# A one-core decoder kernel: clearing the gather buffer in two earlier parts, and storing each tile of h ahead of the preceding tile's normed rows

## The chip, the cores and the metric

The kernel runs on one core of one Trainium2 chip. The metric is the device time of one execution in microseconds (us). TensorE (PE) does the matmuls, VectorE (DVE) and ScalarE (ACT) the work on elements, GpSimd (POOL) issues the indirect transfers that gather and scatter rows, and SyncE (SP) issues nearly all other transfers. The engines run apart and meet only at semaphores. All arrays are float32 unless a name says otherwise.

## What is computed

Two layers over 512 positions of 1024 channels. Layer 0 mixes by windowed attention and a short convolution, layer 1 by trailing means; each mixer is followed by a mixture of 16 experts, of which a position uses two. Cut to what matters here:

```python
for layer in range(2):
    u = rms_norm(h, norm_mix[layer]) * (1 + sc1) + sh1
    h = h + g1 * mix(u)                       # attention + convolution, or pooling
    u = rms_norm(h, norm_ffn[layer]) * (1 + sc2) + sh2
    h = h + g2 * grouped_moe(u, ...)          # sigmoid scores, best group, top 2 of it
return rms_norm(h, norm_final)
```

```python
def grouped_moe(h, ...):
    scores = sigmoid(h @ w_router)            # 16 experts in 4 groups
    ...                                       # best group, its two best experts, gates
    for e in range(16):
        hid = silu(t @ w_gate[e]) * (t @ w_up[e])
        out = out + gates[:, e:e + 1] * (hid @ w_down[e])
```

## The kernel before

The 512 positions are T = 4 tiles of 128 partitions. `h` holds the residual in SBUF, `xhat` the rows divided by their root mean square. In each layer the work goes: mixer, norm, router, routing, expert loop, adding back.

**Mixer and norm.** In layer 0 TensorE multiplies attention and convolution outputs by `w_out` (`mix_half(t, a)`, tile t, half a of the columns, 16 matmul records each) and raises `mix_banked` after each half: it reads 6 when tile 2 is done and 8 when tile 3 is. VectorE adds a half to `h` (`mix_in`, L1033 and L1034); with the second half of a tile it raises `h_ready`. In layer 1 `pool_in` (L1049) does this. ScalarE sums the squares of the finished row (`norm`, L708), VectorE or, for the last tile in layer 0 and the last two in layer 1, ScalarE (`last_tile`, L745) scales it into `xhat` and raises `xhat_ready`.

**Stores.** SyncE writes both `h` and `xhat` to device memory (`h_dram`, `xhat_dram`), since the experts' rows are gathered from `xhat_dram` and their outputs added into `h_dram`. It does so tile by tile (L499 to L502), in the order of its program: it waits for `xhat_ready`, stores the tile of `h`, then the tile of `xhat`, 512 KB each. `xhat_stored` counts the `xhat` stores that have landed. POOL issues no gather before all four have.

**Routing.** `route(l)` on VectorE starts with a CAST of token numbers into a bfloat16 table (L1190), waits for ScalarE's sigmoid (L743), and goes through a chain of short operations (L1194 to L1224) to the choice of experts. TensorE turns that into positions (L1809); `one_hots` (L1312) and `tokens` (L1322, L1331) make the list of rows of the first experts and raise `table_ready`. `keep_clock` (L1547) are matmuls on constants whose result nobody reads, put between these steps.

**Gather.** POOL gathers an expert's rows from `xhat_dram` into one of four buffers of `xg` (L626, indirect, up to 128 rows); row numbers out of bounds write nothing, so `xg` is cleared once, by a MEMSET of 128x4096 (L594) behind the loads of the modulation vectors (`load_gate`, `load_cols`, L554 to L564), which POOL issues once `h_ready` counts four tiles. `xg` lies in the same SBUF columns of `work` as `convT` and `attnT`, the left operands of the mix: column block t*128 to (t+1)*128 of each of their eight rows of 512 is what the mix of tile t reads.

**Expert loop.** TensorE transposes the gathered rows (`turn_in`, L1854), ScalarE (L847) and VectorE (L1394) copy them out with scale and shift, TensorE multiplies (L1877, L1915). Expert weights come through four slots, freed as TensorE goes on; those of experts 0 and 1 are loaded ahead, the rest only when VectorE has sorted the experts (`ids_ready`). In layer 0 SyncE in addition waits for the gather of expert 1. Outputs are scattered (L613, L607) into `h_dram`.

Of the kernel before, what the change touches and what calls it, by code (L numbers as in the profile page):

```python
# [30 lines left out]
P = 128  # L31
SEQ, D = 512, 1024
T = SEQ // P
# [44 lines left out]
def trunk(nc, x, c, w_ada, b_ada, norm_mix, norm_ffn, w_in, w_out, sinks, conv_w, w_pool, pool_scale,  # L78
          w_router, b_router, w_gate, w_up, w_down, norm_final, consts, pool_mats, out, mod_dram, xhat_dram, h_dram):
    ctx = ExitStack()  # L80
    with ctx:
        ctx.enter_context(nc.allow_non_contiguous_dma(reason="vectors of 1024 channels, 128k + p at partition p"))

        def sb(name, shape, dt=F32):
            return ctx.enter_context(nc.sbuf_tensor(name, shape, dt))

        def sem(name):
            return ctx.enter_context(nc.semaphore(name))


        h = sb("h", [P, T, D])
        xu = sb("xu", [P, 2 * T * D])
        xhat = xu[:, 0:T * D].rearrange("p (t d) -> p t d", t=T)
# [37 lines left out]
        def take(n):  # L131
            at[0] += n
            assert at[0] <= WORK, at[0]
            return work[:, at[0] - n:at[0]]
# [18 lines left out]
        xg = take(4 * D).rearrange("p (b d) -> p b d", b=4)  # L153
# [120 lines left out]
        std_done, xhat_ready = sem("std_done"), sem("xhat_ready")  # L274
        xhat_stored = sem("xhat_stored")
# [5 lines left out]
        h_part, h_ready = sem("h_part"), sem("h_ready")  # L281
# [11 lines left out]
        mix_banked = sem("mix_banked")  # L293
# [7 lines left out]
        xg_clear = sem("xg_clear")  # L301
# [6 lines left out]
        h_stored = sem("h_stored")  # L308
# [105 lines left out]
        def _(sp):  # L414
# [81 lines left out]
            sp.dma_start(psc, pool_scale.partition_broadcast(P).rearrange("p a d -> p (a d)")).then_inc(wpool_in, 16)  # L496
            for l in range(LAYERS):

                for t in range(T):  # L499
                    sp.wait_ge(xhat_ready, (2 * l + 1) * T + t + 1)  # L500
                    sp.dma_start(h_dram[l][t * P:(t + 1) * P, :], h[:, t, :]).then_inc(h_stored, 16)
                    sp.dma_start(xhat_dram[l][t * P:(t + 1) * P, :], xhat[:, t, :]).then_inc(xhat_stored, 16)  # L502
                if l == 0:

                    sp.wait_ge(mix_banked, 2 * T)
                    load_expert(0, 1, 1, parts="g")
                if l == 0:

                    sp.wait_ge(xg_in[1], 16)

                sp.wait_ge(xhat_stored, 16 * T * (l + 1))
                sp.wait_ge(logits_ready, 2 * (l + 1))
                sp.wait_ge(ids_ready, l + 1)
                chosen = {}
                for e in range(FIXED, E):
                    chosen[e] = sp.value_load(ids[0:1, e - FIXED:e - FIXED + 1], min_val=0, max_val=E - 1)
                    if e < NSLOT:
                        load_expert(l, e, e % 4, chosen[e])
                        continue

                    load_expert(l, e, e % 4, chosen[e], parts="gu")
                    if e > NSLOT:
                        load_expert(l, e - 1, (e - 1) % 4, chosen[e - 1], parts="d")
                load_expert(l, E - 1, (E - 1) % 4, chosen[E - 1], parts="d")
                overflow_sync(sp, l)

                for j in range(2):
                    sp.wait_ge(y_out[j], 16 * SCATTERS[j] * (l + 1))  # L528
                for t in range(T):
                    sp.dma_start(h[:, t, :], h_dram[l][t * P:(t + 1) * P, :]).then_inc(h_in[t], 16)  # L530
                if l == 0:

                    for t in range(T):
                        sp.wait_ge(h_in[t], 16 * 2)
                    for e in range(FIXED):
                        load_expert(1, e, e)
# [7 lines left out]
        def _(pool):  # L544
            def load_cols(s):

                l, half = s // 2, s % 2
                mod_waits(pool, PIECES.index((l, 3 * half + 1)))
                off = 3 * half * D

                for a in range(s == 2, 2):
                    src = mod_dram[l, off + a * D:off + (a + 1) * D]
                    src = src.rearrange("(k p) -> p k", p=P) if s == 2 else src.rearrange("(p k) -> p k", k=KD)
                    pool.dma_start(modc[:, s, a, :], src).then_inc(modc_in[s], 16)  # L554
                if half:

                    for a in range(2):
                        pool.dma_start(modk[:, l, a, :], mod_dram[l, off + a * D:off + (a + 1) * D]
                                       .rearrange("(k p) -> p k", p=P)).then_inc(modc_in[s], 16)

            def load_gate(l, half):
                off = (3 * half + 2) * D
                mod_waits(pool, PIECES.index((l, 3 * half + 2)))
                pool.dma_start(gbc[:, :] if half else gmix[l], mod_dram[l:l + 1, off:off + D].partition_broadcast(P)  # L564
                               .rearrange("p a d -> p (a d)")).then_inc(gbc_in, 16)
# [11 lines left out]
            for l in range(LAYERS):  # L577
                if l == 0:
                    load_cols(1)

                pool.wait_ge(h_ready, T * (l + 1))
                load_gate(l, 1)
                if l:
# [7 lines left out]
                    load_gate(1, 0)  # L591

                if l == 0:
                    pool.memset(xg[:, :, :], 0.0).then_inc(xg_clear, 1)  # L594
                    pool.wait_ge(xg_clear, 1)
                pool.wait_ge(xhat_stored, 16 * T * (l + 1))

                def scatter(e):
# [1506 lines left out]
```

## Time and profile before

| what | value |
|---|---|
| three timed runs, median | 689.59 us |
| lowest and highest of them | 689.57 and 692.98 us |
| profiled execution, its time | 691.79 us |
| its span, first to last instruction | 690.1 us |
| mean granted clock of TensorE | 0.965 of full |
| TensorE busy | 636.4 us, 92% |
| VectorE busy | 358.3 us, 52% |
| ScalarE busy | 171.5 us, 25% |
| POOL busy | 96.9 us, 14% |
| gather of expert 0 issued, layer 0 and layer 1 | 273.57 us and 499.98 us |

Start times count from the start of the span of the profiled execution. The profiled execution lies 2.2 us above the median of the timed runs, and 1.7 us of its time lie outside its span. TensorE is near full but for two stretches of some 15 us, from 264 and from 490 us, where routing runs on VectorE and the gathers are awaited.

### The profile page before, as it was taken

What the parts mean: (1) busy time and instruction counts of PE and PEld (TensorE: products, weight loads), DVE (VectorE), ACT (ScalarE), POOL (GpSimd) and SP (SyncE); (2) the same over time, 40 slices, a digit from 0 to 9 for tenths busy, and PEclk for the clock granted to TensorE, in tenths of its full rate; (3) what the DMA queues carried; (4) which work ended last, traced back from release to release, by engine and by line L of the source; (5) the groups of instructions that cost most, each with busy time, mean ns of one, the idle gap of its engine ahead of it and who ended that gap; (6) DMA issues with size and microseconds to landing.
All of it is one profiled execution on the core that took longest, in us unless ns stands there. A gap on an engine that the chain in (4) does not pass through costs nothing. (4 is left out here: it accounts for less than half of the span.)

```text
span 690.1 us, 8415 instructions
## 1 busy us (share of the span) xinstructions
PE 636.4 (92%) x2897; PEld 328.6 (48%) x2897; DVE 358.3 (52%) x714; ACT 171.5 (25%) x437; POOL 96.9 (14%) x84
## 2 busy tenths in 40 slices
PE   4899989999899995889999999999678999999994
PEld 3455434444444442445455554468345455555441
DVE  4117698799996237863432222264776233223325
ACT  5000322323333421211122211242421122122223
POOL 0010001000000004113132312100021212222210
PEclk9999989999999996989999999999989999999997
DMA  9999998878889415799999998374789899999726
GB/s 326 361 367 371 384 318 289 328 263 293 311 307 393 160 64 186 249 410 312 322 345 371 359 321 272 92 274 183 305 304 393 278 309 354 370 367 364 253 41 244
DMA packets 68568, 203.76 MB, mean 295 GB/s; under 512 B 9633, under 2 KB 18965, under 8 KB 68524
## 3 DMA queue, kind: packets, MB, share of 16 engines
q1 hardware_dynamic: 58836, 183.63, 72.3%
q0 software_dynamic: 9040, 18.87, 11.4%
q10 hardware_dynamic: 648, 0.71, 0.3%
q8 instruction: 24, 0.39, 0.2%
q14 instruction: 20, 0.16, 0.1%
HBM read 189.90 MB, written 23.11 MB: 309 GB/s over the span
## 5 line engine op out<-in xcount | busy, mean ns | idle before, releaser
L1877 PE MATMUL ps<-ring,work 128*128 128x512 f32 x288 | 127.8, 595 | 0.0
L949 DVE SCALAR_TENSOR_TENSOR acc<-adaw,cond,acc 128x1024 f32<-128x1024 f32 x70 | 89.8, 1283 | 8.5 <-DMA adaw<-in_w_ada_dram 6.6
L1701 PE MATMUL psY<-xu,ring 128*128 128x512 f32 x192 | 88.0, 612 | 0.0
L1877 PEld LDWEIGHTS ps<-ring,work 128*128 128x128 f32 x288 | 54.3, 191 | 67.1 <-issue 66.8
L1402 DVE TENSOR_TENSOR work<-work,ps 128x256 f32<-128x256 f32 (+1 forms) x32 | 11.9, 372 | 128.6 <-ACT work L854 92.7
L854 ACT ACTIVATE work<-ps 128x256 f32<-128x256 f32 (+1 forms) x32 | 11.0, 344 | 237.7 <-PE ps L1877 175.6
L1915 PE MATMUL psY<-ring,work 128*128 128x512 f32 x144 | 69.8, 630 | 0.0
L1701 PEld LDWEIGHTS psY<-xu,ring 128*128 128x128 f32 x192 | 36.4, 195 | 45.4 <-issue 45.2
L613 POOL DMA_INDIRECT h_dram<-work x20 | 33.2, 1662 | 152.7 <-DVE work L1432 75.4
L847 ACT ACTIVATE work<-psA,modc,scl 128x128 f32<-128x128 f32 (+1 forms) x120 | 42.5, 434 | 48.2 <-PE psA L1854 46.6
L1432 DVE SCALAR_TENSOR_TENSOR work<-psY,work,gbc 128x512 f32<-128x512 f32 x40 | 28.2, 747 | 44.1 <-PE psY L1915 44.1
L1394 DVE TENSOR_SCALAR work<-psA,scl,modc 128x128 f32<-128x128 f32 (+1 forms) x120 | 37.8, 377 | 14.9 <-PE psA L1854 13.3
L626 POOL DMA_INDIRECT work<-xhat_dram,work x32 | 34.6, 1081 | 67.9 <-DVE work L1331 33.0
L1760 PE MATMUL psY<-ring,work 128*128 128x512 f32 x96 | 42.8, 597 | 0.8 <-DVE h L1034 0.8
L1915 PEld LDWEIGHTS psY<-ring,work 128*128 128x128 f32 x144 | 27.6, 202 | 28.9 <-issue 28.6
L1854 PE MATMUL psA<-cst,work 128*128 128x128 f32 (+1 forms) x240 | 34.3, 281 | 5.2 <-DMA work<-xhat_dram,work 5.2
L1854 PEld LDWEIGHTS psA<-cst,work 128*128 128x128 f32 (+1 forms) x240 | 30.7, 196 | 10.8 <-DMA work<-xhat_dram,work 7.0
L564 POOL DMA_DIRECT2D gbc<-mod_dram x3 | 1.7, 572 | 219.3 <-DVE h L1034 140.7
L791 ACT ACTIVATE work<-work,sm 128x256 f32<-128x256 f32 (+1 forms) x32 | 15.0, 471 | 52.6 <-DVE sm L1116 52.6
L1760 PEld LDWEIGHTS psY<-ring,work 128*128 128x128 f32 x96 | 17.7, 190 | 21.8 <-issue 21.8
L708 ACT ACTIVATE work<-h 128x1024 bf16<-128x1024 f32 x19 | 20.0, 1050 | 14.3 <-DVE h L1357 12.6
L1868 PE MATMUL ps<-ring,work 128*64 128x256 f32 x192 | 23.0, 390 | 0.0
(266 smaller groups left out, 782.1 us busy)
## 6 DMA issues: line engine op xcount, KB each, us to landing
adaw<-in_w_ada_dram SPq DMA_DIRECT2D x84, 512.0 KB, 5.3
ring<-in_w_gate_dram SPq DMA_DIRECT2D x48, 512.0 KB
ring<-in_w_up_dram SPq DMA_DIRECT2D x48, 512.0 KB
ring<-in_w_down_dram SPq DMA_DIRECT2D x48, 512.0 KB
xu<-in_w_gate_dram SPq DMA_DIRECT2D x16, 512.0 KB
xu<-in_w_up_dram SPq DMA_DIRECT2D x16, 512.0 KB
xu<-in_w_down_dram SPq DMA_DIRECT2D x16, 512.0 KB
work<-in_w_ada_dram SPq DMA_DIRECT2D x12, 512.0 KB, 9.9
```

The source lines that it names most:

```text
L613: pool.indirect_dma_start(out=h_dram[l], out_offset=bass.IndirectOffsetOnAxis(tok_i[:, e:e + 1], 0), in_=yrow[:, e % 2, :], in_offset=None ...
L626: pool.indirect_dma_start(out=xg[0:rows, e % 4, :], out_offset=None, in_=xhat_dram[l], in_offset=bass.IndirectOffsetOnAxis(tok_i[0:rows, e ...
L847: ins = act.activation(xgT[:, j % 2, k, 0:n], turned_ps(e)[:, k * P:k * P + n], ACT.Identity, scale=scl[:, 2 * l + 1, k:k + 1], bias=modc[ ...
L949: dve.scalar_tensor_tensor(total, adaw[:, n % ABUF, :], cond[:, k:k + 1], total if k else brow[:, :], ALU.mult, ALU.add).then_inc(mac_step, 1)
L1394: ins = dve.tensor_scalar(xgT[:, j % 2, k, 0:n], turned_ps(e)[:, k * P:k * P + n], scl[:, 2 * l + 1, k:k + 1], modc[:, 2 * l + 1, 0, k:k + 1],
L1432: ins = dve.scalar_tensor_tensor(yrow[:, j % 2, cols], psY[:, cols], gslot[:, bass.ds(e, 1)], gbc[:, cols], ALU.mult, ALU.mult)
L1701: ins = pe.matmul(bank, wt, uT[:, k, :], start=(k == 0), stop=(k == KD - 1))
L1760: ins = pe.matmul(ps[:, a * 512:(a + 1) * 512], lhs, wo[:, q, a * 512:(a + 1) * 512], start=(q == 0), stop=(q == 7))
L1854: ins = pe.transpose(turned_ps(e)[:, k * P:k * P + n], xg[0:n, j % 4, :].rearrange("p (a k) -> p k a", k=KD)[:, k, :], ident[0:n, 0:n])
L1868: ins = pe.matmul(gu_ps[j % 2][q * H64:(q + 1) * H64, 0:FF] .rearrange("p (a f) -> p a f", a=2), xgT[:, j % 2, k, 0:H64], w_gu(j % 4)[:, : ...
L1877: ins = pe.matmul(gu_ps[j % 2][:, :].rearrange("p (a f) -> p a f", a=2), xgT[:, j % 2, k, :], w_gu(j % 4)[:, :, k, :], start=(k == 0), sto ...
L1915: ins = pe.matmul(psY[:, a * 512:(a + 1) * 512], hT[:, q, :], w_dn(j)[:, q, a * 512:(a + 1) * 512], start=(q == 0), stop=(q == 1))
```

## The change

POOL now clears `xg` in two parts, ahead of the loads that wait for `h_ready`: 3072 columns of a partition (the blocks of tiles 0 to 2, eight rows of 384) when `mix_banked` reads 6, and the other 1024 (eight rows of 128) when it reads 8. SyncE stores a tile of `h` when that tile's `h_ready` is up, one step ahead of the `xhat` tile before it: h0, h1, xhat0, h2, xhat1, h3, xhat2, xhat3. This loop serves both layers.

```diff
-                for t in range(T):
-                    sp.wait_ge(xhat_ready, (2 * l + 1) * T + t + 1)
-                    sp.dma_start(h_dram[l][t * P:(t + 1) * P, :], h[:, t, :]).then_inc(h_stored, 16)
-                    sp.dma_start(xhat_dram[l][t * P:(t + 1) * P, :], xhat[:, t, :]).then_inc(xhat_stored, 16)
+                for t in range(T + 1):
+                    if t < T:
+                        sp.wait_ge(h_ready, l * T + t + 1)
+                        sp.dma_start(h_dram[l][t * P:(t + 1) * P, :], h[:, t, :]).then_inc(h_stored, 16)
+                    if t:
+                        sp.wait_ge(xhat_ready, (2 * l + 1) * T + t)
+                        sp.dma_start(xhat_dram[l][(t - 1) * P:t * P, :], xhat[:, t - 1, :]).then_inc(xhat_stored, 16)
...
                 if l == 0:
                     load_cols(1)
 
+                    parts = xg.rearrange("p b d -> p (b d)").rearrange("p (c s) -> p c s", s=SEQ)
+                    pool.wait_ge(mix_banked, 2 * (T - 1))
+                    pool.memset(parts[:, :, 0:(T - 1) * P], 0.0).then_inc(xg_clear, 1)
+                    pool.wait_ge(mix_banked, 2 * T)
+                    pool.memset(parts[:, :, (T - 1) * P:SEQ], 0.0).then_inc(xg_clear, 1)
                 pool.wait_ge(h_ready, T * (l + 1))
                 load_gate(l, 1)
...
                 if l == 0:
-                    pool.memset(xg[:, :, :], 0.0).then_inc(xg_clear, 1)
-                    pool.wait_ge(xg_clear, 1)
+                    pool.wait_ge(xg_clear, 2)
                 pool.wait_ge(xhat_stored, 16 * T * (l + 1))
```

POOL's instructions in layer 0 before, from the loads of layer 0's first modulation vectors (`modk`, L558) on to the first gather:

```order
L558 DMA modk<-mod_dram 128x8x1 x2
L564 DMA gbc<-mod_dram 128x1024 [waits mod_stored0,mod_stored1,h_ready]
L554 DMA modc<-mod_dram 128x8x1 [waits mod_stored0,mod_stored1]
L554 DMA modc<-mod_dram 128x8 [waits mod_stored1,mod_stored0]
...
L564 DMA acc<-mod_dram 128x1024 [waits mod_stored0,mod_stored1]
L594 MEMSET work 128x4096
L626 DMA work<-xhat_dram,work 128x1024 [waits table_ready,xhat_stored,xg_clear]
```

The same place after the change, where L567 and L633 are the lines that were L564 and L626:

```order
L561 DMA modk<-mod_dram 128x8x1 x2
L586 MEMSET work 128x8x384 [waits mix_banked]
L588 MEMSET work 128x8x128 [waits mix_banked]
L567 DMA gbc<-mod_dram 128x1024 [waits mod_stored0,mod_stored1,h_ready]
...
L567 DMA acc<-mod_dram 128x1024 [waits mod_stored0,mod_stored1]
L633 DMA work<-xhat_dram,work 128x1024 [waits table_ready,xhat_stored,xg_clear]
```

Between the last load and the first gather POOL has nothing left to do; the clearing stands ahead of the first instruction that waits for `h_ready`.

SyncE's stores in layer 0 before, behind the loads of the pooling weights (L494 to L496) and ahead of a part of expert 1's weights (L454); the pair L501, L502 stands four times:

```order
L494 DMA adaw<-in_w_pool_dram 128x8x256 [waits mac_step]
L495 DMA adaw<-pool_matrices 128x1152
L496 DMA adaw<-in_pool_scale_dram 128x1024
L501 DMA h_dram<-h 128x1024 [waits xhat_ready]
L502 DMA xhat_dram<-xu 128x1024
...
L454 DMA ring<-in_w_gate_dram 128x1024 [waits mix_banked]
```

And after (L502 is now the store of `h`, L505 that of `xhat`):

```order
L496 DMA adaw<-in_pool_scale_dram 128x1024
L502 DMA h_dram<-h 128x1024 [waits h_ready] x2
L505 DMA xhat_dram<-xu 128x1024 [waits xhat_ready]
L502 DMA h_dram<-h 128x1024 [waits h_ready]
...
L505 DMA xhat_dram<-xu 128x1024 [waits xhat_ready] x2
L454 DMA ring<-in_w_gate_dram 128x1024 [waits mix_banked]
```

The last tile of `xhat` has no store of `h` directly ahead of it any more.

## Rows read from the trace of the kernel before

**Rows 1.** Timeline, layer 0 routing: start, duration (us), engine, line, operation [idle, releaser].

```profile
259.78 1.77 POOL L558 DMA_DIRECT2D modk<-mod_dram  x2
260.82 4.92 DVE L1190 CAST work<-cst 128x128 bf16<-128x128 f32 x1
261.23 4.52 DVE L1194 TENSOR_TENSOR work<-sig_tile,brb 128x64 f32<-128x64 f32 x1
261.55 0.56 POOL L564 DMA_DIRECT2D acc<-mod_dram  x1
262.10 3.53 POOL L594 MEMSET work<- 128x4096 f32 x1
...
272.47 0.16 DVE L1331 SCALAR_TENSOR_TENSOR work<-work 128x1 uint32<-128x1 f32 x1
273.57 1.09 POOL L626 DMA_INDIRECT work<-xhat_dram,work  x1 [7.95 <-DVE work L1331]
...
275.41 1.02 POOL L626 DMA_INDIRECT work<-xhat_dram,work  x1 [0.76 <-DVE work L1331]
...
280.14 1.16 PE L1854 MATMUL psY<-cst,work 128*128 128x128 f32 x8 [1.13 <-DMA work<-xhat_dram,work]
```

**Rows 2.** Timeline, layer 1: a load by POOL, routing, a store, two gathers.

```profile
481.96 0.60 POOL L584 DMA_DIRECT2D acc<-in_norm_final_dram  x1
...
482.30 0.77 DVE L955 TENSOR_SCALAR xu<-h,rstd 128x1024 f32<-128x1024 f32 x1
...
488.28 0.25 DVE L1190 CAST work<-cst 128x128 bf16<-128x128 f32 x1
488.69 0.22 DVE L1194 TENSOR_TENSOR work<-sig_tile,brb 128x64 f32<-128x64 f32 x1 [0.16 <-ACT sig_tile L743]
...
491.34 1.21 SPq L502 DMA_DIRECT2D xhat_dram<-xu  x1
...
495.61 0.16 DVE L1331 SCALAR_TENSOR_TENSOR work<-work 128x1 uint32<-128x1 f32 x1
...
499.98 1.05 POOL L626 DMA_INDIRECT work<-xhat_dram,work  x1 [17.43 <-DMA xhat_dram<-xu]
...
501.34 1.03 POOL L626 DMA_INDIRECT work<-xhat_dram,work  x1 [0.30 <-issue]
...
506.17 1.91 PE L1854 MATMUL psY<-cst,work 128*128 128x128 f32 x8
```

**Rows 3.** Landing of the last store of xhat, layer 0 first, then layer 1.

```profile
L502 SPq DMA_DIRECT2D xhat_dram<-xu x1: 432/432/432, 262.6 to 262.6; - x1
DMA to landing us min/median/max: 6.5/6.5/6.5
...
DMA to landing us min/median/max: 7.9/7.9/7.9
```

**Rows 4.** Windows: stretch, length, busy us by engine, TensorE clock, DMA share, GB/s.

```profile
478.00:480.00 2.00, 2.00 (x14) 1.75 (x12) 1.28 (x2) 1.38 (x2) 0.00 (x0) 1.00 0.00 0
...
494.00:496.00 2.00, 0.89 (x5) 0.61 (x6) 1.50 (x6) 0.00 (x0) 0.00 (x0) 0.75 1.01 414
...
501.00:502.00 1.00, 0.00 (x0) 0.00 (x0) 0.90 (x4) 0.00 (x0) 0.69 (x2) 0.92 0.31 37
502.00:503.00 1.00, 0.00 (x0) 0.00 (x0) 0.44 (x2) 0.00 (x0) 0.37 (x1) 0.50 0.30 90
```

**Rows 5.** Timeline, layer 0, around the mix of tiles 2 and 3.

```profile
245.00 0.69 DVE L1033 TENSOR_TENSOR xu<-psY,gbc 128x512 f32<-128x512 f32 x1 [5.47 <-PE psY L1760]
...
255.55 0.69 DVE L1033 TENSOR_TENSOR xu<-psY,gbc 128x512 f32<-128x512 f32 x1 [3.90 <-PE psY L1760]
...
257.26 0.56 POOL L564 DMA_DIRECT2D gbc<-mod_dram  x1 [140.66 <-DVE h L1034]
```

**Rows 6.** Timeline, layer 0: second products of expert 0 and of expert 1.

```profile
301.77 6.41 PE L1915 MATMUL psY<-ring,work 128*128 128x512 f32 x8
...
316.01 3.60 PE L1915 MATMUL psY<-ring,work 128*128 128x512 f32 x8
```

## The prediction, made before the changed kernel was run

> **What bounds the kernel now.** I first read the busy shares: TensorE is busy 92% of the span, so only its gaps and its slow stretches are to be had. The windows along the span put the two largest gaps where routing runs, at 264 us in layer 0 and at 490 us in layer 1. So I read the timeline of these two places beside each other; the same instructions run in both.
>
> In layer 0 the CAST that opens the routing takes 4.92 us and the TENSOR_TENSOR behind it 4.52 us; both end at 265.75 us, 0.12 us behind the end of POOL's MEMSET at 265.63 [rows 1]. In layer 1, where POOL issues nothing at that time, the same two take 0.25 and 0.22 us [rows 2]. The reader is to see a VectorE held by POOL. What follows is a chain on VectorE up to the list of rows of expert 0 (start 272.47 us), and the gather starts 0.94 us behind its end [rows 1]. Here the chain on VectorE ends last.
>
> In layer 1 this list is ready at 495.77 us, but the gather starts at 499.98 us, released by a store of `xhat` [rows 2]. Issued at 491.34 us and landing 7.9 us later, at 499.24 us [rows 2, 3], this last store ends last there. In layer 0 it landed at about 269.1 us (262.6 + 6.5) [rows 3], while the list came at 272.63 us: hidden by 3.5 us.
>
> **The clearing, layer 0.** It takes away a MEMSET of 3.53 us between 262.10 and 265.63 us. What VectorE gains has two bounds. If only the MEMSET held it, the CAST would end near 261.1 us and the TENSOR_TENSOR, which starts at 261.23 us, at 261.23 + 0.22 = 261.45 us: a gain of 265.75 - 261.45 = 4.3 us. But the CAST started 1.28 us before the MEMSET's row begins, five times its length in layer 1. What POOL did in that time were the loads L558 and L564, up to 262.11 us [rows 1]. If their descriptors hold VectorE as well, it is free 0.11 us behind them, at 262.2 us: a gain of 3.5 us. Against this stands a TENSOR_SCALAR of layer 1 that started at 482.30 us and took 0.77 us, beside a load that POOL was issuing until 482.56 us [rows 2]: had it waited for that end, it would have taken longer. I take 3.5 us, by the row of the CAST itself, and keep 4.3 for the range.
>
> The Trainium skill (SBUF — State Buffer, section "Who interferes with whom") says that a VectorE cast in a two-port mode and any GpSimd operation exclude each other for a whole instruction, the first to issue winning, and that GpSimd needs the same port while it writes descriptors. By that rule the loads ahead of the MEMSET keep the CAST waiting, which is the 3.5 us; that a MEMSET took the port ahead of a CAST that had been waiting for it is more than the rule tells, and the trace shows it.
>
> The parts must go somewhere. At 3.53 us for 4096 columns the first (3072) costs 2.65 us and the second (1024) 0.88 us, if rows of 384 and 128 cost POOL nothing more. The first starts when the mix of tile 2 is read, at about 237.3 us. VectorE is then in `mix_in` of tile 2 and `turned_half`; were it held throughout, those end 2.65 us later, and VectorE had 5.47 us with nothing to do before 245.00 us [rows 5]. Cost zero; without that cover 2.65 us. The second starts with `mix_in` of tile 3 at 255.55 us and would end by 256.6 us, while POOL's next instruction waited for `h_ready` until 257.26 us [rows 5]. POOL's loads, queued behind it, keep their times, and the gather behind them has the whole of VectorE's chain as cover. But `mix_in` of tile 3 is on the path (norm, router and the CAST follow). It costs between 0 and 0.9 us. I take 0: these are not casts, and the forms of VectorE in that place (PSUM beside SBUF) ran at their usual 0.69 us beside POOL's loads too. The skill's same section states that a VectorE operation with two SBUF inputs is held only by a GpSimd operation that reads SBUF; a MEMSET reads nothing, so by the page 0 as well, and no row of this trace shows it alone.
>
> With 3.5 us less, the list is ready at 269.1 us and the gather starts at 270.0 us. The `xhat` store must not be late then: it landed at 269.1 us [rows 3], and POOL started 0.74 us behind the landing in layer 1 (499.24 to 499.98). So without the other edit it would be just in time; with it, 512 KB less stand in front, and it is early. SyncE's wait for expert 1's gather and for the sorted ids moves with VectorE, so the weights of experts 2 and 3 come 3.5 us earlier too. Nothing else in layer 0 has a fixed time; the weights of experts 0 and 1 are there long before. **Layer 0: 3.5 us.**
>
> **The stores, layer 1.** Tiles 0 and 1 of `h` are finished while TensorE is still mixing tiles 2 and 3, and the transfer engines move nothing then (0 GB/s from 478 to 480 us); their stores move there. Ahead of the last landing the engines run full (414 GB/s from 494 to 496 us, share 1.01) [rows 4]: bytes set the landing. Before, six of the eight stores and two loads of 512 KB (POOL's) had been issued by 490 us; after, two stores of `h` (0, 1) have landed, and of the rest `xhat` 0 and 1 and `h` 2 and 3 have been issued. That is as much in the queue as before. But behind it come only `xhat` 2 and 3, where `h` 2, `xhat` 2, `h` 3 and `xhat` 3 came. 1.05 MB less at 414 GB/s is 2.5 us. The last store lands at 496.7 instead of 499.24 us, and the gather starts 0.74 us behind, at 497.45 us. The list (495.77 + 0.94 = 496.7 us) allows that, but hardly more: this is what is late next. The second gather starts 1.36 us behind the first, at 498.8 us; where lists release them the two are 1.84 us apart (273.57 and 275.41), which allows it from 496.7 + 1.84 = 498.5 us [rows 1, 2].
>
> The second gather's transposes started 4.73 us behind its issue in layer 0 (280.14 - 275.41), where TensorE waited for it. So they start at 503.5 us. They took 1.16 us there and 1.91 us in layer 1 (from 506.17 us) [rows 1, 2]: TensorE's granted clock had fallen to half just before, at about 501.9 us, 2.1 us into an idle stretch [rows 4]. They end at 504.7 us at full clock or 505.4 us at half, against 508.08 us: a gain of 3.4 or 2.6 us. The new idle stretch is also some 2 us long, so I take the middle, 3.0 us. The transposes release everything that follows: VectorE's copies, the lists of experts 2 and up, the first product. The weights of expert 2 are asked for at 503.3 us as before (the sort doesn't wait for a gather), but its product comes behind all of experts 0 and 1. **Layer 1: 3.0 us.**
>
> **Nothing.** In layer 0 the stores of `h` 0 and 1 go out behind the pooling weights, which are wanted only in the expert loop; `xhat` 2 waits behind `h` 3 until 257 us, and has 12 us. The second layer has no clearing. Two more instructions on POOL cost under 0.3 us of its idle time.
>
> **Sum.** 3.5 + 3.0 = 6.5 us. The profiled execution took 691.79 us and would take 685.3; it lies 2.2 us above the median of the timed runs (689.59), from which I forecast 683.1 us.
>
> **Rivals.**
> - *VectorE comes free at once.* The CAST doesn't wait for descriptors: 4.3 + 3.0 to 3.4 us, 682.3 to 681.9 us. For it: the TENSOR_SCALAR at 482.30 us; against it: the CAST's early start.
> - *Only one of the two gains comes.* If the CAST waits for something that stays (POOL's loads, and then the next of them), layer 1 alone gives 686.6 us. If the last `xhat` store lands no earlier, since the engines share out their time between all that is queued and not in order, layer 0 alone gives 686.1 us. Against it: the landings of layer 0 and 1 differ as the bytes in front of them do.
> - *The second part holds `mix_in` of tile 3.* 0.9 us on the path, and POOL's loads start as much later, so VectorE comes free 0.9 us later: 2.6 + 3.0 us, 684.0 us.
> - *The clearing in rows is slow.* A POOL MEMSET of short rows has no row in this trace. If rows of 384 and 128 cost f times the column rate, the second part ends at 237.3 + 3.53 f us once the first is the longer. POOL's loads (5 us) then start there and not at 257.26 us, and hold the CAST as they do now. At f = 5.7 that begins; at f = 6.6 layer 0 gains nothing, and at f = 7.5 layer 1's 3.0 us are gone too. Beyond it is slower than before: at f = 9 the loads come 11.8 us late, 5.3 us more than both gains, 694.9 us.
> - *TensorE's clock.* Stretches at half clock have other places when the gaps move. Expert 0's second product in layer 0 took 6.41 us where expert 1's took 3.60 [rows 6]. One such stretch more or less is 2.8 us: 680.3 or 685.9 us.
>
> **How the numbers follow.** A measurement of this kernel can tell about 0.5%, 3.4 us, from no change. Forecast (both gains, within 1.5 us of the sum): 0.50. VectorE free at once: 0.15. Only one gain: 0.15. Second part holds `mix_in`: 0.07. Slow clearing: 0.03. Clock: 0.10, half each way. Faster by over 0.5% (below 686.1 us) are the forecast, the free VectorE, the held `mix_in`, most of the clock and a third of the single gains: 0.83. Within 0.5%: 0.14. Slower: 0.03. The range goes from 680.0 us (clock one way, free VectorE) to 687.0 us (one gain).
>
> **What would show it.** Right: in layer 0 the CAST ends by 262.3 us and the first gather starts near 270 us; a MEMSET of 128x8x384 takes about 2.7 us from 237 us; in layer 1 the first gather starts near 497.5 us less the shift of layer 0 (494 us in the new trace), and the last `xhat` store lands in 5.4 us rather than 7.9. Wrong: a CAST that still takes microseconds, a MEMSET part of 5 us or more, `mix_in` of tile 3 longer than 1.4 us, a landing unchanged in layer 1, or expert loops that take longer between the first transpose and the last scatter than before, which would say that the gain is given back there.

## The result, and the profile after

Over 11 timed runs each, the kernel after took 684.59 us in the median (680.33 to 687.97) and the kernel before 692.98 (689.57 to 698.38). The ratio is 0.9894, with a 95% interval from 0.9869 to 0.9920 (the plain quotient of the two medians, 0.9879, lies inside it): 1.06%, some 7.3 us (5.5 to 9.1), are gone. The forecast was 683.1 us and a gain of 6.5. The range held the time, and the gain is clear of the noise. The profiled execution has a span of 686.3 us against 690.1 and a mean granted clock of 0.971 against 0.965.

Timeline of the kernel after, layer 0, from the last addition to `h` to the second gather's transposes. The columns are as in [rows 1], whose lines it answers to. Line numbers have moved: L1197 is the CAST, L1201 the operation behind it, L561 and L567 are loads of POOL, L633 the gather.

```profile
258.28 0.95 POOL L588 MEMSET work<- 128x1024 f32 x1 [15.63 <-PE psY L1767]
258.98 0.69 DVE L1041 TENSOR_TENSOR h<-h,xu 128x512 f32<-128x512 f32 x1
...
262.49 1.78 POOL L561 DMA_DIRECT2D modk<-mod_dram  x2
...
263.45 0.25 DVE L1197 CAST work<-cst 128x128 bf16<-128x128 f32 x1
...
263.86 0.23 DVE L1201 TENSOR_TENSOR work<-sig_tile,brb 128x64 f32<-128x64 f32 x1 [0.16 <-ACT sig_tile L750]
...
270.76 0.16 DVE L1338 SCALAR_TENSOR_TENSOR work<-work 128x1 uint32<-128x1 f32 x1
...
271.87 1.08 POOL L633 DMA_INDIRECT work<-xhat_dram,work  x1 [7.05 <-DMA xhat_dram<-xu]
...
278.59 1.16 PE L1861 MATMUL psY<-cst,work 128*128 128x128 f32 x8 [1.39 <-DMA work<-xhat_dram,work]
```

The CAST takes 0.25 us where it took 4.92 [rows 1], and this although it lies beside a load (L561) that POOL is still issuing. The CAST waits for no semaphore. So that the engines meet only at semaphores, as is said at the start, is not the whole: here POOL held VectorE without one. The second part of the clearing lies over the last addition to `h`, which keeps its 0.69 us. The gather is now released by the landing of a store, though the list was ready at 270.92 us.

The same kernel in layer 1, answering to [rows 2]; below it the landing of the last `xhat` store there, answering to the last line of [rows 3]:

```profile
479.04 0.69 DVE L1056 TENSOR_TENSOR h<-h,psY 128x512 f32<-128x512 f32 x1 [0.88 <-PE psY L1806]
...
488.42 1.36 SPq L505 DMA_DIRECT2D xhat_dram<-xu  x2
...
494.30 0.16 DVE L1338 SCALAR_TENSOR_TENSOR work<-work 128x1 uint32<-128x1 f32 x1
...
496.44 1.06 POOL L633 DMA_INDIRECT work<-xhat_dram,work  x1 [15.19 <-DMA xhat_dram<-xu]
...
497.80 1.02 POOL L633 DMA_INDIRECT work<-xhat_dram,work  x1 [0.30 <-issue]
...
500.77 1.16 PE L1861 MATMUL psA<-cst,work 128*128 128x128 f32 x8 [1.22 <-DMA work<-xhat_dram,work]
...
502.74 1.97 PE L1861 MATMUL psY<-cst,work 128*128 128x128 f32 x8 [0.81 <-DMA work<-xhat_dram,work]
```

```profile
L505 SPq DMA_DIRECT2D xhat_dram<-xu x1: 320/320/320, 489.5 to 489.5; - x1
...
DMA to landing us min/median/max: 6.2/6.2/6.2
```

Absolute times of two executions can't be compared here. The one after reached the last addition to `h` in layer 0 at 258.98 us, the one before at 256.27, and nearly all of that lag was there before the first changed instruction ran, the store of `h` 0 at 219.78 us (the third half of the mix started at 208.31 us against 205.63). So everything below is counted within a layer, from the start of the last addition to `h`. A + is such a distance in us. The table has one profiled execution of each kernel; the last column of a layer is the end of the second gather's transposes, which release all that follows.

| kernel | L0: CAST takes | L0: first gather | L0: transposes end | L1: first gather | L1: transposes end |
|---|---|---|---|---|---|
| before | 4.92 | +17.30 | +25.03 | +19.63 | +27.73 |
| after | 0.25 | +12.89 | +20.77 | +17.40 | +25.67 |
| clearing alone | 0.25 | +13.76 | +22.05 | +19.85 | +29.50 |
| stores alone | 4.68 | +17.30 | +24.69 | +17.02 | +24.49 |
| one early MEMSET | 0.25 | +13.09 | +21.40 | +17.20 | +25.02 |
| POOL's loads behind the gathers | 0.25 | +12.89 | +20.37 | +16.31 | +25.36 |
| the same, weights ahead | 0.25 | +14.94 | +23.44 | +16.30 | +24.26 |

In the two profiled executions layer 0 gains 25.03 - 20.77 = 4.3 us and layer 1 gains 27.73 - 25.67 = 2.1 us. Between them (from the end of these transposes to the last addition of layer 1) both take nearly the same: 199.0 us before and 199.3 after. No more than 0.2 to 0.3 us is given back in the expert loop.

### The profile page after: what moved, and what is told of

Its sections match the earlier page's. It is cut to its first block and busy times, and to the rows that moved or that the text cites. A ratio compares the mean times of both kernels' runs of the same rounds, so it can differ in the third digit from the quotient of the medians.

```text
span 686.3 us, 8416 instructions
## 1 busy us (share of the span) xinstructions
PE 638.0 (93%) x2897; PEld 328.7 (48%) x2897; DVE 353.9 (52%) x714; ACT 171.6 (25%) x437; POOL 97.0 (14%) x85
## 5 line engine op out<-in xcount | busy, mean ns | idle before, releaser
L633 POOL DMA_INDIRECT work<-xhat_dram,work x32 | 34.6, 1080 | 65.0 <-DVE work L1338 24.5
L1875 PE MATMUL ps<-xu,work 128*64 128x256 f32 x192 | 22.9, 388 | 0.0
```

Source lines behind the costliest of these rows:

```text
L633: pool.indirect_dma_start(out=xg[0:rows, e % 4, :], out_offset=None, in_=xhat_dram[l], in_offset=bass.IndirectOffsetOnAxis(tok_i[0:rows, e ...
L1875: ins = pe.matmul(gu_ps[j % 2][q * H64:(q + 1) * H64, 0:FF] .rearrange("p (a f) -> p a f", a=2), xgT[:, j % 2, k, 0:H64], w_gu(j % 4)[:, : ...
```

## The experiments

Seven of the runs below were timed in one execution each (the MEMSET over the CAST, the later first part, the added MEMSET, the added wait and the three cut MEMSETs). Only their rows are used; nothing is concluded from their total times.

### Each edit alone

The clearing alone keeps the two early MEMSETs and takes back the loop of stores (shown against the kernel after):

```diff
-                for t in range(T + 1):
-                    if t < T:
-                        sp.wait_ge(h_ready, l * T + t + 1)
...
+                for t in range(T):
+                    sp.wait_ge(xhat_ready, (2 * l + 1) * T + t + 1)
+                    sp.dma_start(h_dram[l][t * P:(t + 1) * P, :], h[:, t, :]).then_inc(h_stored, 16)
+                    sp.dma_start(xhat_dram[l][t * P:(t + 1) * P, :], xhat[:, t, :]).then_inc(xhat_stored, 16)
```

> Clearing in two early parts alone, stores as before. Theory (the MEMSET held the CAST, POOL's loads don't): the CAST takes 0.25 us, the chain from its start to the next operation behind it 0.67 us instead of 4.97, and the first gather of layer 0 starts 13.0 us (list) to 13.6 us (landing of the last xhat store plus 0.74) behind the last h addition of the mix, against 17.3 before and 12.9 with both edits. Layer 1 stays at 19.6 us from its last h addition to the first gather. Sum 3.7 to 4.3 us, ratio 0.994. Rival (the stores carry the gain of layer 0 too, since the last xhat store lands late behind the h store): first gather at over 14.5 us, ratio 0.996 or more. Rival of the prediction (POOL's loads hold the CAST): the CAST ends about 1.1 us behind its start, 3.5 us gained.

Measured: ratio 0.9968 (0.9945 to 0.9990), so 2.2 us, and the expected 0.994 lies just outside the interval. From this run, with the CAST (L1194) beside the same load (L558) and the gather (L630):

```profile
259.84 1.78 POOL L558 DMA_DIRECT2D modk<-mod_dram  x2
260.79 0.25 DVE L1194 CAST work<-cst 128x128 bf16<-128x128 f32 x1
...
268.11 0.16 DVE L1335 SCALAR_TENSOR_TENSOR work<-work 128x1 uint32<-128x1 f32 x1
...
270.09 1.09 POOL L630 DMA_INDIRECT work<-xhat_dram,work  x1 [7.92 <-DMA xhat_dram<-xu]
```

The CAST took 0.25 us, and the next operation but one started 0.67 us behind its start and not 4.97. The first gather came at +13.76 us, 0.16 us beyond what was expected, held by the landing of the last `xhat` store, while its list was ready at +11.94. Layer 1's first gather came at +19.85 us, near the +19.63 of before. So the clearing frees VectorE by 4.3 us, of which this run's gather got 3.5 us, and the transposes 3.0, since TensorE ran them mostly at half clock (1.90 and 1.69 us where they take 1.16). In layer 1 the profiled execution then lost 1.8 us: its transposes ended at +29.50 us against +27.73, though nothing is changed there.

The stores alone are the reverse: the kernel before with the new loop, of which this is the wait that moves.

```diff
...
-                    sp.wait_ge(xhat_ready, (2 * l + 1) * T + t + 1)
+                        sp.wait_ge(h_ready, l * T + t + 1)
...
```

> The stores' new order alone, clearing as before. Theory (fewer bytes in front of the last xhat store in layer 1): first gather of layer 1 17.4 us behind the last h addition instead of 19.6, layer 0 unchanged at 17.3 with a CAST of some 4.9 us; 2.0 to 2.5 us, ratio 0.997. Rival (the two edits help each other, or the gain of layer 1 came from elsewhere): layer 1 unchanged, ratio 1.000; or both layers gain.

Measured: ratio 0.9955 (0.9933 to 0.9976), 3.1 us. Layer 0's first gather stayed at +17.30 us; layer 1's came at +17.02, 2.6 us earlier, and its transposes ended 3.2 us earlier, both at full clock. The single gains (2.2 and 3.1 us) add up to 2.0 us less than the 7.3 us of both. The intervals of the three ratios allow that difference to be none, and they also allow the 0.9 us in layer 0 that the clearing alone loses to the late store.

### What held the CAST

Three runs take the MEMSET by itself. In the first, one MEMSET of all columns stands directly behind the wait for `h_ready`, ahead of POOL's loads, with the new stores and without the two early parts:

```diff
                 pool.wait_ge(h_ready, T * (l + 1))
+                if l == 0:
+                    pool.memset(xg[:, :, :], 0.0).then_inc(xg_clear, 1)
                 load_gate(l, 1)
```

> New order of the stores, and one MEMSET of 4096 columns directly behind the wait for h_ready, ahead of POOL's loads, in place of two parts. It runs for 3.5 us and ends as the CAST starts. Theory (all that counts is that no MEMSET lies over the CAST; POOL's loads, now 3.5 us later and beside the CAST and what follows, hold nothing): CAST 0.25 us or up to 0.5 if it catches the MEMSET's tail, same time as with two parts within 0.5 us, ratio 0.989 to 0.991. Rival (the loads hold VectorE when they lie beside the routing, or other VectorE operations beside the MEMSET are held): VectorE operations from 0.3 us behind the last h addition on are longer, 1 to 3.5 us of the gain gone.

Measured: ratio 0.9897 (0.9865 to 0.9929), not told apart from the 0.9894 with two parts. The MEMSET ran from 257.03 to 260.54 us and the CAST started at 260.95 and took 0.25 us, beside loads of POOL. Splitting the clearing is not what pays; having it off the CAST is.

The second starts the same MEMSET when the first router scores are banked, so that it lies over the CAST and no load is near (shown against the run before):

```diff
                 if l == 0:
+                    pool.wait_ge(score_banked, 1)
                     pool.memset(xg[:, :, :], 0.0).then_inc(xg_clear, 1)
```

> New order of the stores; one MEMSET of 4096 columns, ahead of POOL's loads, that POOL starts when the first router scores are banked, so some 0.8 us ahead of the CAST and with no load near. Theory (a MEMSET by itself holds the CAST for as long as it runs): CAST ends 0.11 us behind the MEMSET, takes 2.7 to 3.0 us; the operations of VectorE ahead of the CAST keep their 0.17 and 0.23 us. Rival (only the loads hold; what looked like the MEMSET was their work going on): CAST 0.25 us.

Timeline of this run, POOL and VectorE around the CAST (L1195):

```profile
258.30 3.51 POOL L587 MEMSET work<- 128x4096 f32 x1 [142.41 <-PE ps L1672]
258.42 0.52 DVE L1029 SCALAR_TENSOR_TENSOR sig_tile<-ps,rstd,work 128x16 f32<-128x16 f32 x3
...
259.20 2.73 DVE L1195 CAST work<-cst 128x128 bf16<-128x128 f32 x1
259.60 2.32 DVE L1199 TENSOR_TENSOR work<-sig_tile,brb 128x64 f32<-128x64 f32 x1
261.75 0.56 POOL L567 DMA_DIRECT2D gbc<-mod_dram  x1
```

The MEMSET ends at 261.81 us and the CAST at 261.93. So a MEMSET that is under way holds a CAST to its end without any load. The operations from PSUM ahead of the CAST are not held (0.52 us, as in the kernel before), and the TENSOR_TENSOR behind it ends with it.

The third asks which other forms are held. It is the kernel after, with the first part of the clearing waiting for one more half of the mix:

```diff
-                    pool.wait_ge(mix_banked, 2 * (T - 1))
+                    pool.wait_ge(mix_banked, 2 * (T - 1) + 1)
```

> Both edits, with the first part of the clearing (3072 columns) released one half of a mix later, so that it lies over VectorE's TENSOR_TENSOR of two SBUF operands (the h addition) and over the TENSOR_SCALAR of the norm of tile 2 (SBUF to SBUF, 0.75 us alone). Theory (a MEMSET holds casts and scalings from SBUF to SBUF, and no operation of two operands or from PSUM): the h addition keeps 0.69 us, the TENSOR_SCALAR ends 0.1 us behind the MEMSET where it starts inside it, up to 1.4 us long; nothing on the path, the first gathers as with both edits. Rival (only the CAST, by its form, is held): TENSOR_SCALAR 0.75 us.

```profile
245.63 2.66 POOL L586 MEMSET work<- 128x3072 f32 x1 [129.32 <-PE psY L1767]
246.33 0.69 DVE L1041 TENSOR_TENSOR h<-h,xu 128x512 f32<-128x512 f32 x1
246.94 0.68 DVE L1006 COPY xu<-ps 128x512 f32<-128x512 f32 x1
247.54 0.15 DVE L961 RECIPROCAL rstd<-rstd 128x1 f32<-128x1 f32 x1
247.73 1.10 DVE L962 TENSOR_SCALAR xu<-h,rstd 128x1024 f32<-128x1024 f32 x1
```

The timeline shows the TENSOR_TENSOR and the COPY from PSUM at their usual times in the midst of the MEMSET, and the TENSOR_SCALAR at 1.10 us instead of 0.75. It ended 0.54 us behind the MEMSET and not the 0.1 that was expected; its own work is longer than that of a CAST (0.75 against 0.25 us), which may be why. The form that keeps its time is also the one that is on the path in the kernel after: the addition of tile 3. The Trainium skill (SBUF — State Buffer, section "Who interferes with whom") states that a VectorE operation with two SBUF inputs contends with a GpSimd operation that reads SBUF and not with one that only writes it. The trace agrees: the addition took 0.69 us inside the MEMSET, as without it.

That leaves the 1.28 us in which the CAST of [rows 1] was held before the row of the MEMSET began. Five runs bear on it. In the first, POOL clears one buffer a second time at the old place:

```diff
+                if l == 0:
+                    pool.wait_ge(xg_clear, 2)
                 pool.wait_ge(h_ready, T * (l + 1))
...
-                    pool.wait_ge(xg_clear, 2)
+                    pool.memset(xg[:, 3, :], 0.0).then_inc(xg_again, 1)
+                    pool.wait_ge(xg_again, 1)
```

> Both edits, and in addition a MEMSET of 1024 columns at the old place behind POOL's loads. It asks what held the CAST in the 1.28 us before the MEMSET's row began. Theory A (a MEMSET that is queued behind POOL's loads takes the port ahead of its row's start, or holds a CAST that is under way): the CAST ends some 0.1 us behind the end of this MEMSET of 0.95 us, so takes about 2.3 us. Theory B (POOL's loads or something else of that execution held it, and the MEMSET only from its row's start): the CAST takes 0.25 us, since it is over before the MEMSET's row begins.

```profile
260.49 1.77 POOL L561 DMA_DIRECT2D modk<-mod_dram  x2
...
261.20 1.15 DVE L1200 CAST work<-cst 128x128 bf16<-128x128 f32 x1
261.61 0.75 DVE L1204 TENSOR_TENSOR work<-sig_tile,brb 128x64 f32<-128x64 f32 x1
262.25 0.56 POOL L567 DMA_DIRECT2D acc<-mod_dram  x1
...
262.80 0.97 POOL L604 MEMSET work<- 128x1024 f32 x1
```

Neither theory holds as it was put: the CAST was held, but only to 262.35 us, 0.09 us behind L561 and 0.45 us ahead of the MEMSET's row. The same kernel without this MEMSET but with the added wait was to move POOL's loads 0.24 us against VectorE and to do nothing else:

> Both edits, and POOL waits once more (for the clears) ahead of its loads, which shifts the loads by some 0.25 us against VectorE and does nothing else. In the run with the short MEMSET the CAST started 0.71 us into the two loads of L561 and took 1.15 us, ending 0.10 us behind them and ahead of the MEMSET; with both edits alone it started 0.96 us into them and took 0.25. Theory A (the loads hold the CAST when it falls on certain parts of them): CAST again near 1.1 us without any MEMSET behind. Theory B (the MEMSET in the queue did it): CAST 0.25 us.

```profile
259.96 1.78 POOL L561 DMA_DIRECT2D modk<-mod_dram  x2
...
261.14 0.69 DVE L1199 CAST work<-cst 128x128 bf16<-128x128 f32 x1
261.55 0.29 DVE L1203 TENSOR_TENSOR work<-sig_tile,brb 128x64 f32<-128x64 f32 x1
261.74 0.56 POOL L567 DMA_DIRECT2D acc<-mod_dram  x1
```

The loads moved by 0.24 us, but the CAST came 0.47 us later as well (+4.94 us against +4.47), for a reason that was not looked for, and so fell 1.18 us into L561 and not 0.7. It was held again, 0.69 us in all, to 0.09 us behind L561. So loads alone can hold a CAST. But they did so in one of the six executions in which the CAST met them without a MEMSET behind. In the other three runs the kernel before has its MEMSET cut, which leaves the rest of `xg` uncleared:

```diff
-                    pool.memset(xg[:, :, :], 0.0).then_inc(xg_clear, 1)
+                    pool.memset(xg[:, 3, :], 0.0).then_inc(xg_clear, 1)
```

> The kernel before with its MEMSET cut to 1024 of 4096 columns (three of the four gather buffers stay uncleared). The CAST falls on the loads as in the kernel before. Theory A (caught on the loads, the CAST loses the port again to what POOL has queued, down to the end of the MEMSET): it ends 0.1 us behind the end of the MEMSET, so takes 2.3 us (4.92 less 2.6). Theory B (only the loads hold it, and what happens in the MEMSET's time is another thing): it ends 0.1 us behind the loads, 0.8 to 1.4 us. Theory C (the CAST is not caught at all in this run, as its place against the loads differs): 0.25 us.

With `xg[:, 0:2, :]`, 2048 columns:

> The kernel before with its MEMSET cut to 2048 of 4096 columns (two gather buffers stay uncleared). In the kernel before and in the run with the new stores alone the CAST ended 0.11 us behind the end of the full MEMSET; with 1024 columns it ended 0.09 us behind the loads L558. Theory A (the port goes from the loads to the MEMSET when the MEMSET is long): CAST ends 0.1 us behind the end of the MEMSET of 1.8 us, takes some 3.2 us. Theory B (only the loads hold it unless the MEMSET has all 4096 columns): ends 0.1 us behind L558, 0.5 to 1.2 us.

With the first 1536 columns:

> The kernel before with its MEMSET cut to 1536 of 4096 columns (the rest stays uncleared). Counted from the start of the loads L558, the CAST came free at 1.87 us with no MEMSET or one of 1024 columns (0.1 us behind L558), at 2.42 us with 2048 (0.1 us behind the next load), at 5.96 us with 4096 (0.1 us behind the MEMSET). Theory A (part of POOL works ahead of the rows: it starts the MEMSET some 0.6 us into L558 and holds the port for the MEMSET's length): free at 0.6 + 1.4 + 0.1 = 2.1 us, behind no row's end. Theory B (the port is given away only at the end of one of POOL's instructions, and which one depends on the MEMSET's size): 1.87 or 2.42 us.

Counted from the start of the loads of `modk` (L558 before, L561 after; they end at 1.77 to 1.85 us, the next load 0.56 us later), all executions in which the CAST met them:

| MEMSET queued behind | CAST starts at | free at | behind the end of |
|---|---|---|---|
| 4096 columns (before; stores alone) | 1.04; 1.28 | 5.96; 5.96 | the MEMSET, 0.11 |
| 2048 | 0.95 | 2.42 | the next load, 0.09 |
| 1536 | 0.96 | 1.92 | L558, 0.15 |
| 1024 (cut; added) | 1.38; 0.71 | 1.87; 1.86 | L558 or L561, 0.09 |
| none (added wait) | 1.18 | 1.87 | L561, 0.09 |
| none (after, clearing alone, two more) | 0.95 to 0.96 | at once | |
| none (first part later) | 1.13 | at once | |

With a MEMSET in POOL's queue the CAST was held in six of six executions, always before the MEMSET's row had begun. With 1024 columns it came free at 1.86 and 1.87 us, just as with none and the added wait: those two may be the loads' doing alone. With 1536 and 2048 columns it was held from 0.96 and 0.95 us, where without a MEMSET it went through four times. That speaks for the queued MEMSET acting ahead of its row, on two executions against four.

The last run was to decide between 2.1 us (part of POOL works on the MEMSET ahead of its row) and 1.87 or 2.42 us (the CAST comes free at the end of a row of POOL). It gave 1.92, nearer to the second. With the start of the MEMSET's work set afterwards to 0.45 us, the first still fits: 0.45 + 1.84 + 0.1 = 2.4 us for 2048 columns and 0.45 + 1.40 + 0.1 = 1.95 for 1536. These are the rows of the run with 2048:

```profile
260.04 1.78 POOL L558 DMA_DIRECT2D modk<-mod_dram  x2
260.99 1.47 DVE L1190 CAST work<-cst 128x128 bf16<-128x128 f32 x1
261.81 0.56 POOL L564 DMA_DIRECT2D acc<-mod_dram  x1
262.36 1.84 POOL L594 MEMSET work<- 128x2048 f32 x1
```

The CAST was free at 262.46 us, as the row of its MEMSET began, and was not held by that row, while with 4096 columns it was held through the whole row. The first reading has the port released 0.03 us ahead of that row, and then a row of full length all the same. The second fits all seven held executions to within 0.06 us (0.09 to 0.15 us behind some row's end), but does not say why a longer MEMSET makes it a later row. Neither is shown, and this point stays open. What is shown is that the full MEMSET cost the CAST its length of 3.53 us and 0.9 to 1.1 us more.

### What sets the landing of the last store

In layer 1, POOL's two loads of 512 KB go behind the gathers of experts 0 and 1:

```diff
+                    if l and e == 1:
+                        pool.wait_ge(h_ready, T * (l + 1))
+                        load_gate(l, 1)
+                        pool.dma_start(nfin, norm_final.rearrange("(a d) -> a d", a=1).partition_broadcast(P)
+                                           .rearrange("p a d -> p (a d)")).then_inc(nfin_in, 16)
                     if e >= 4:
                         scatter(e - 4)
```

> Both edits, and POOL's two loads of 512 KB in layer 1 (gate row and final norm) are issued behind the gathers of experts 0 and 1 instead of ahead of them. Theory (in layer 1 the bytes in front of the last xhat store set its landing): 1.05 MB less in front, the store lands up to 2.5 us earlier, and the list of expert 0 now releases the gather, 16.4 us behind the last h addition instead of 17.4 (19.6 before the change); the second transposes end 0.5 to 1.2 us earlier, ratio to before 0.988. Rival (landing goes by something else than bytes, such as the store's own share of the queues): the gather still waits for the xhat store, at 17.2 us or more.

```profile
L505 SPq DMA_DIRECT2D xhat_dram<-xu x1: 319/319/319, 487.7 to 487.7; - x1
...
DMA to landing us min/median/max: 3.1/3.1/3.1
```

Measured: the landing takes 3.1 us, after 6.2 with both edits and 7.9 before [rows 3], for 1.05 MB less in front each time. The steps are not equal (1.7 and 3.1 us), but what stands in front decides: over all runs, the landing in layer 1 took 7.8 to 8.1 us with the old order, 5.8 to 6.4 with the new, and 3.1 in the two runs with POOL's loads behind. The list now releases the gather, at +16.31 us, as expected. Of these 1.1 us little arrives: the second gather waits for its own list (+18.23 us), and its transposes ended at +25.36 us, 0.3 us earlier, where 0.5 to 1.2 were expected. The ratio of 0.9861 (0.9814 to 0.9908) is not told apart from 0.9894.

The next run has this and, in layer 0, expert 1's gate weights ahead of the last two `xhat` stores:

```diff
+                    if t == T - 1 and l == 0:
+                        load_expert(0, 1, 1, parts="g")
                     if t:
                         sp.wait_ge(xhat_ready, (2 * l + 1) * T + t)
```

> As the run before, and in layer 0 the 1 MB of expert 1's gate weights is asked for ahead of the last xhat store and not behind it. Theory (in layer 0 the last xhat store, which landed 6.1 us behind its issue with both edits, shares the engines with those weights and with the scattered loads of POOL): its landing takes 4.5 us or less, the list alone releases the first gather, at 12.9 us behind the last h addition as before; no more than 0.3 us over the run before, ratio 0.988. Rival (the weights now in front delay it): landing 6 us or more and a first gather over 13.5 us.

```profile
L507 SPq DMA_DIRECT2D xhat_dram<-xu x1: 327/327/327, 262.3 to 262.3; - x1
...
  POOL work L629: 9.1, 1
...
DMA to landing us min/median/max: 8.1/8.1/8.1
```

The theory fell and the rival came true: 1 MB in front cost 2.0 us of landing (8.1 against 6.1 us) and the same on the gather, +14.94 us against +12.89. The ratio was 0.9879 (0.9826 to 0.9931); the 2 us in layer 0 are within the noise of the timed runs but plain in the trace. What is issued ahead of the store counts, also in layer 0. Two runs above show it from the other side: where POOL's loads went out later, the store in layer 0 landed in 4.6 us (MEMSET directly behind the wait for `h_ready`) and in 2.9 us (MEMSET over the CAST, all of POOL's loads behind the store).

## Why the prediction was right, point by point

**The clearing, layer 0: the cause right, the size too small.** That the MEMSET held VectorE was right. The forecast took 3.5 us between 3.5 and 4.3, by the CAST's early start, holding that POOL's loads would go on holding it. Measured: 4.3 us from the CAST's start to the start of the next operation but one (4.97 against 0.67), so the first rival, "VectorE comes free at once", came true in layer 0. The step that failed is "I take 3.5 us, by the row of the CAST itself". What was right in it is that the loads can hold the CAST (the run with the added wait). What was wrong is that they mostly don't: in five of six executions without a MEMSET the CAST went through. The rule of the Trainium skill (SBUF — State Buffer, section "Who interferes with whom") beside which the forecast was set, that whoever issues first gets the shared ports, does not cover what was seen: a CAST whose row begins 1.28 us ahead of the MEMSET's still came behind it.

**Where the parts went: right.** The parts took 2.66 and 0.95 us (forecast 2.65 and 0.88), and 1024 columns in a single row took 0.97 us in two other runs, so the division into eight rows costs nothing. Both operations of `mix_in` for tile 3 kept their 0.69 us beside the second part (for the one from PSUM the forecast had no row beside POOL's loads: what ran there at 0.69 us was a COPY from PSUM), and POOL's loads began 0.99 us behind the start of that addition, as before. The rivals "the second part holds `mix_in`" and "the clearing in rows is slow" are out.

**The `xhat` store in layer 0: too optimistic.** The forecast had it early with 512 KB less in front. It landed 6.1 us behind its issue (before: 6.5), at 271.0 us, just when the list was ready, and the profile names it as the releaser in the kernel after. In the new order `xhat` 2 goes out 4.8 us ahead of it, where it went out 14.4 us ahead; that may be why the missing store of `h` brought only 0.4 us. It cost nothing here, but the clearing alone lost 0.9 us to it: 1.8 us between list and gather, where the list alone needs 0.9. So the order of the stores is needed for the full gain of the clearing; the margin that was expected was not there.

**The stores, layer 1: right in mechanism and nearly in size.** The landing was to take 5.4 us instead of 7.9, from the same issue. It took 6.2 us from an issue that lay 0.5 us earlier, so the store landed 2.2 us earlier and not 2.5. (The forecast's list of the queue has `h` 2 and `xhat` 2 twice, as issued by 490 us and as still to come; its sum of 1.05 MB less is right.) In the five executions with the old order (before, clearing alone, the three cut MEMSETs) the first gather came at +19.6 to +19.9 us; in seven with the new one and nothing else changed in layer 1 at +17.0 to +17.6. That is 2.4 us. The transposes were to give 2.6 or 3.4 us depending on TensorE's clock.

The transposes ended at +27.5 to +31.2 us in the old order and at +24.0 to +25.7 in the new: 2.9 us earlier by the medians, near the forecast's 3.0, and 3.9 us by the means (28.8 and 24.9), since two of the five old ones end late, at +29.5 and +31.2. In these two the second gather itself came late: its transposes start 6.3 and 7.95 us behind its issue, against 4.8 to 4.9 in the other three and 4.1 to 5.0 in the seven. What may delay it is traffic: in the old order SyncE asks for the weights of experts 2 and 3 1.7 to 2.0 us behind the second gather's issue, in the seven 4.1 to 4.7 us. But all five have these weights close behind and only two were late, so this is argued and not shown. From the run with 1024 columns (old order):

```profile
497.82 1.15 POOL L626 DMA_INDIRECT work<-xhat_dram,work  x1 [0.30 <-issue]
499.51 0.90 SPq L454 DMA_DIRECT2D ring<-in_w_gate_dram  x2
...
505.77 1.97 PE L1854 MATMUL psY<-cst,work 128*128 128x128 f32 x8 [2.91 <-DMA work<-xhat_dram,work]
```

And from the run with the stores alone (new order):

```profile
498.22 1.02 POOL L629 DMA_INDIRECT work<-xhat_dram,work  x1 [0.30 <-issue]
...
502.89 0.90 SPq L454 DMA_DIRECT2D ring<-in_w_gate_dram  x2
503.17 1.16 PE L1857 MATMUL psY<-cst,work 128*128 128x128 f32 x8 [0.88 <-DMA work<-xhat_dram,work]
```

The transposes start 7.95 us behind the gather's issue in the one and 4.95 us in the other. The ids that release the weights don't wait for the gather, so an earlier gather goes out further ahead of them.

**TensorE's clock.** It was said to decide between 2.6 and 3.4 us in layer 1. With both edits the second transposes ran at half clock (1.97 us), behind idle stretches of 1.2 us (not the 2 us of the forecast) and 0.8 us, with the stores alone at full (1.16 us), behind 0.65 and 0.9 us. Their ends, counted from the last addition, lie 1.2 us apart: 0.8 us of that is the clock, and 0.4 us is an earlier start.

**The sum.** In the two profiled executions 4.3 and 2.1 us are gained and 0.2 to 0.3 us are given back in between; in the timed runs 7.3 us (5.5 to 9.1) are gained. The forecast's 6.5 was made of one term that was 0.8 us too small and another, 3.0 us, that was 0.9 us too large in this pair of executions and about right by the medians of five and seven. That the errors cancel in the pair is luck, and the timed interval is too wide to tell more. The median itself came out 1.5 us above 683.1 although the gain was larger, because eight more runs of the kernel before moved its median from 689.59 to 692.98 us.

## What to carry to other kernels

When a short VectorE operation takes microseconds in one place and a fraction of one in another, look at what POOL has in its queue, and not only at the row beside it. In this kernel a clearing cost nothing where VectorE read PSUM or two operands, and microseconds over a cast; whether it was one instruction or two made no difference that could be told. Where a consumer waits for the last of several stores, order the queue by what is ready first: in layer 1 every 512 KB taken from in front brought the landing 0.8 to 1.6 us forward. Ask also what moves close to it instead: in layer 0 the new order brought 0.4 us.

## What the hardware showed that was not expected

- A MEMSET on POOL held a CAST of VectorE to 0.11 or 0.12 us behind its own end, with no semaphore between them: 4.92, 4.68 and 2.73 us where the CAST takes 0.25.
- The CAST was held before the row of the MEMSET began in six of six executions with a MEMSET queued behind POOL's loads, and in one of six without (0.44 us more, by loads). In the two with 1024 columns the loads alone explain it.
- A TENSOR_SCALAR of 1024 columns from SBUF to SBUF, caught by a MEMSET, took 1.10 us instead of 0.75; an addition of two SBUF operands and a COPY from PSUM kept their 0.69 us.
- A MEMSET on POOL costs by its columns: 3.53, 2.66, 1.84, 1.40 and 0.95 to 0.97 us for 4096, 3072, 2048, 1536 and 1024 float32 columns, whether in one row or in eight.
- The same store of 512 KB took 2.9 to 8.1 us to land, by what was issued in front of it.
